# The first latent product issued before the change of blocks, in a decoder step on one core

## The reference

```python
def sq_relu_mlp(x, w_up, w_down):
    h = jax.nn.relu(x @ w_up)
    return (h * h) @ w_down

def shared_kv(h, pos, norm_kv, w_dkv, kv_norm, w_kr):
    hn = rmsnorm(h, norm_kv)
    ckv = rmsnorm(hn @ w_dkv, kv_norm)
    krope = rope(hn @ w_kr, pos)
    return ckv, krope
...
        h = h + sq_relu_mlp(rmsnorm(h, p["norm_mlp"][layer]), p["w_up"][layer], p["w_down"][layer])
        if layer == N_A_LAYERS - 1:
            ckv, krope = shared_kv(h, pos, p["norm_kv"], p["w_dkv"], p["kv_norm"], p["w_kr"])
```

## Time and profile before

| | us |
|---|---|
| median of 3 runs | 2909.66 |
| lowest and highest | 2902.77 and 2913.35 |
| the profiled execution | 2903.06 |
| its span in the trace | 2901.3 |
| TensorE busy in the span | 2766.8 (95%) |
| VectorE, ScalarE, GpSimd busy | 1455.0, 800.2, 736.6 |
| mean granted TensorE clock | 0.984 of full |

### The profile page before, as it was taken

The page is one execution under the profiler, slowest core; times in us unless marked ns, Lnnn a source line. Parts: engine busy times, 40 slices in busy tenths (PEclk is TensorE's granted clock), DMA queues, the critical chain, the costliest instruction groups (busy, mean ns, idle before and its releaser), DMA issues. The chain is left out here.

```text
span 2901.3 us, 54265 instructions
## 1 busy us (share of the span) xinstructions
PE 2766.8 (95%) x22530; PEld 2622.4 (90%) x22530; DVE 1455.0 (50%) x2072; ACT 800.2 (28%) x1349; POOL 736.6 (25%) x533
## 2 busy tenths in 40 slices
PE   6999999989899999999998999899999999999998
PEld 5988889978899999999997889767798999999997
DVE  6566666556743433334546666355466444424243
ACT  3122222223434430101213444333234333210101
POOL 2100000013434433333331110012134443333231
PEclk8999999999999999999999999999999999999998
DMA  4111111122233352322111001376222333532221
GB/s 113 46 58 57 54 54 54 45 84 83 84 108 103 106 205 74 103 93 90 38 39 45 31 27 35 127 266 272 67 96 93 111 97 114 185 105 79 103 73 73
DMA packets 244473, 267.48 MB, mean 92 GB/s; under 512 B 26320, under 2 KB 204288, under 8 KB 242208
## 3 DMA queue, kind: packets, MB, share of 16 engines
q1 hardware_dynamic: 208896, 207.34, 21.9%
q0 software_dynamic: 4608, 41.95, 3.7%
q10 hardware_dynamic: 30752, 14.99, 2.0%
HBM read 204.66 MB, written 59.57 MB: 91 GB/s over the span
## 5 line engine op out<-in xcount | busy, mean ns | idle before, releaser
L2083 DVE TENSOR_TENSOR h<-h,G 128x1050 f32<-128x1050 f32 x120 | 149.7, 1248 | 440.8 <-PE G L232 440.8
L232 PE MATMUL G<-a_hi,w_hi 128*128 128x350 f32 x1536 | 331.0, 323 | 0.0
L232 PE MATMUL G<-a_lo,w_hi 128*128 128x350 f32 x1536 | 330.9, 323 | 0.0
L232 PE MATMUL G<-a_hi,w_lo 128*128 128x350 f32 x1536 | 330.4, 323 | 0.0
L171 POOL CAST w_hi<-w_raw 128x1024 fp32r<-128x1024 f32 (+2 forms) x84 | 77.5, 922 | 731.9 <-PEq L1234 477.8
L232 PEld LDWEIGHTS G<-a_hi,w_hi 128*128 128x128 f32 x1536 | 262.8, 189 | 0.0
L232 PEld LDWEIGHTS G<-a_hi,w_lo 128*128 128x128 f32 x1536 | 262.0, 189 | 0.0
L232 PEld LDWEIGHTS G<-a_lo,w_hi 128*128 128x128 f32 x1536 | 261.3, 189 | 0.0
L1784 PE MATMUL G<-T_lo,wS_hi 128*128 128x262 f32 x768 | 219.9, 286 | 10.1 <-DVE T_lo L1940 10.1
L1784 PE MATMUL G<-T_hi,wS_hi 128*128 128x262 f32 x768 | 218.9, 285 | 0.0
L1784 PE MATMUL G<-T_hi,wS_lo 128*128 128x262 f32 x768 | 218.6, 285 | 0.0
(11 more groups left out here) (444 smaller groups left out, 6291.3 us busy)
## 6 DMA issues: line engine op xcount, KB each, us to landing
kept_a<-ring SPq DMA_DIRECT2D x128, 262.0 KB, 2.5
a_raw<-kept_a SPq DMA_DIRECT2D x64, 524.0 KB, 5.5
w_raw<-in_w_down SPq DMA_DIRECT2D x64, 512.0 KB, 3.5
wA_raw<-in_w_up SPq DMA_DIRECT2D x96, 256.0 KB, 3.3
wS_raw<-in_w_up SPq DMA_DIRECT2D x32, 256.0 KB, 3.8
kept_h<-h SPq DMA_DIRECT2D x14, 525.0 KB, 6.3
h<-kept_h SPq DMA_DIRECT2D x14, 525.0 KB, 6.8
w_raw<-in_hg_wq SPq DMA_DIRECT2D x8, 512.0 KB, 4.1
```

The costliest lines, as they stand in the source:

```text
L232: last = nc.tensor.matmul(out, w(a, t), x(b, t, c), start=(t == 0 and (a, b) == ORDER[0]), stop=(t == nk - 1 and (a, b) == ORDER[-1]))
L2083: nc.vector.tensor_tensor(h, h, tile(k, (g0 + t) % 2), ALU.add).then_inc(k.g_free, 1)
```

## The change

The first latent product and its norm product are issued at the end of the feed-forward block, right behind the feed-forward stage's last product, and no longer as the first thing of the `latents` block. GpSimd scales and splits the second latent weight block in the feed-forward block too. The loads of both blocks stood there already. Nothing is added or taken away.

```diff
         split_blocks(k, pool, W_GROUP * GROUPS, n0=self.w0)
         if self.latent_next:
-            split_scaled(k, pool, self.w_next, P, k.g_kv[:, :], k.n_scaled + 1)
+            for j in range(2):
+                split_scaled(k, pool, self.w_next + j, P, k.g_kv[:, :], k.n_scaled + 1 + j)
...
         if self.latent_next:
             pe.wait_ge(k.g_done, self.g_last + KD)
             pe.sem_inc(k.w_used, 1)
+            g = self.g_last + KD
+            first_product(k, pe, self.w_next, g + 1, 0, (g + 1) % 2, act_parts(self.x_hi, self.x_lo), self.x_next,
+                          KD, P, lambda: norm_pe(k, pe, KD, k.rstd, g, self.sq_next))
...
-    assert w0 % 2 == 0 and not k.w_held
+    assert w0 % 2 == 0 and k.w_held
...
-                for j in range(1, 6):
+                for j in range(2, 6):
                     width, gain = ROPE if j == 2 else P, k.g_kv[:, :] if j <= 2 else k.g_mix[:, 1, :]
                     split_scaled(k, pool, w0 + j, width, gain, k.n_scaled + 1 + j)
...
-                first_product(k, pe, w0, g0 + G_C, 0, (g0 + G_C) % 2, x, x0, KD, P,
-                              lambda: norm_pe(k, pe, KD, k.rstd, g0 + G_NORM, sq0))
                 product(1, G_C + 1)
```

## The result

The median is 2916.25 us over 12 runs (2908.55 to 2917.31), before 2909.2 us in the 12 runs of that series; the ratio is 1.0024, 95% interval 1.0014 to 1.0034. So the changed kernel is a little slower and inside the 0.5% that I took for no difference. Two later series of the same two kernels gave 1.0003 (0.9987 to 1.0018) and 1.0007 (0.9996 to 1.0018); both intervals exclude the 1.0024 of the first. Over all 32 runs of the changed kernel the mean is 2913.0 us, over the 76 runs of the kernel before in the same three series 2909.3: **+3.7 us**, with a standard error of 0.8. I had forecast +3.85 and 2913. That the mean comes so close is partly luck: by themselves the three series gave +6.9, +2.1 and +2.3 us.

A forecast was written before the change was run, and what follows sets the result against it. TensorE was busy for 95% of the span, so only its idle time and low clock could change. A later second product, +2.07, and its cold restart, +1.78, made +3.85 us on the median 2909.66: 2913 us, range 2903 to 2919.

The forecast's parts named there:

- The exchange comes later, and ScalarE is ready for the root 7.48 us behind it: Feed-forward block's end: exchange tied to TensorE's end, 1454.06 instead of 1445.08; clears and loads hold the root until 1461.54.
- The first product runs at the full clock after 1.37 us: Feed-forward block's end: TensorE's gap shrinks from 6.41 to 1.37 us; product and norm product take 13.56 us at full clock.
- The second product starts 2.07 us later: Latents block: the second product waits for the root and starts at 1462.87 instead of 1460.80, +2.07 us.
- Cold restart, +1.78: Second latent product: TensorE's 8.8 us idle before it drops the clock, so it starts slowly, +1.78 us.
- The second block's split costs nothing under its cover: Feed-forward block: GpSimd's split delays VectorE by 2.2 us, still ahead of TensorE's need; cost nothing, cover about 3 us.
- Rival 1: Exchange at the feed-forward block's end: TensorE's part doesn't wait for the array, root ready 3.1 us earlier; +0.8 us, chance 0.07.
- Rival 2: Latents block's head: clears and loads don't hold the root; second product follows a 1.6 us gap without clock loss; -5.1 us, chance 0.06.
- So the shift stays: From the second product on: TensorE has no slack to absorb the delay, so the whole +3.85 us remains.

The follow-up runs named there:

- the run that kept the clock up: The changed kernel with 14 useless matmuls on TensorE ahead of the second latent product: 2913.36 us, ratio 1.0013.
- two variants: The changed kernel with the second block's split back in the latents block (2915.29 us, 1.002), and with GpSimd's clears behind its write of rot (2912.95 us, 1.0011).
- The experiment without the cover: The kernel before with only the second latent block's scaling and split moved ahead of the exchange, the product left: 2913.8 us, ratio 1.0019.
- The kernel with the gap of 0.48 us: The changed kernel with the root in the feed-forward block and VectorE's release and reciprocal ahead of its memsets: 2903.72 us, ratio 0.9981.
- its control: The kernel before with the root of the norm ahead of the seven constant loads: 2909.13 us, ratio 0.9999.

## Why the prediction was right, point by point

- *The exchange comes later, and ScalarE is ready for the root 7.48 us behind it.* Right: the loads' last issue ended 1462.21 - 1454.71 = 7.50 us behind the product. Moving the clears made the gap 2.5 us shorter, moving the root in front of the loads made it 7.1 us shorter, and the same edit in the kernel before gave nothing. This step is shown.
- *The first product runs at the full clock after 1.37 us.* Right, 1.39, and in all nine profiles in which the product is moved.
- *The second product starts 2.07 us later.* From the end of the feed-forward stage it was 1460.80 - 1439.13 = 21.67, now 1463.58 - 1439.71 = 23.87: 2.20 later.
- *Cold restart, +1.78.* Right in kind, a little high: 1.58, 1.68 and 1.59 us in the three profiles of the changed kernel, and 1.6 by the run that kept the clock up. The 2.20 of the step above and 1.58 are 3.78, the forecast sum 3.85: the two misses cancel nearly. In two variants, profiled once each, it was 2.43 and 2.84, so the term is not a constant.
- *The second block's split costs nothing under its cover.* Right for the gap, which was 8.87 us with the split in either place. The experiment without the cover gave its price there: the 2.2 us of the gap, some 4.6 in the mean, of which the profile accounts for 4.0.
- *Rival 1, an exchange that doesn't wait for the array.* TensorE's drain of 3.88 us says no once more.
- *Rival 2, the way to a faster kernel.* The mechanism was right and its clock term wrong: with a gap of 1.78 us the cold start stayed. I had priced it at -5.1; the kernel with the root ahead came to 7.0 below the changed kernel, that is -3.3 by the profile. The kernel with the gap of 0.48 us had no cold start.
- *"So the shift stays."* At the place and through the prompt's attention it did. But I had not foreseen that a later block has its own luck with the clock, larger than my sum (1013.3 to 1024.3 us over all profiles). The first series' 1.0024 against the 1.0013 that I had is of that size. That the forecast met the mean of three series is thus partly luck, while the 3.7 us at the place are in all three profiles of the changed kernel. Whether the change itself makes the longer stretches likelier is open. Three profiles of the changed kernel were all at the long end (1023.3, 1023.4, 1024.3), three of the kernel before or its control at 1013.3, 1017.7 and 1021.1. But those three executions are of the changed kernel's upper group, to which only half of its runs belong. The counts lean the same way (6 of 20 and 10 of 12 runs, against 9 of 76) and differ too much between series to show it.

## What to carry to other kernels

Work moved ahead of a point where all engines meet shortens one engine's wait there and uncovers whatever the others have at the head of the next block. Before moving it, list for each engine what it does first behind that point, and for the result that the moved work hands over, how soon its consumer can run: here one square root behind seven load issues decided the sign, and an early root turned +3.7 us into -4.3 and -5.0 (ahead of the loads, two series) and -5.9 (in the feed-forward block), as means. A gap on TensorE costs its length and, in these profiles behind 1.78 us and behind 6.4 to 8.9 us, a slow restart too; the gaps of 0.48, 1.39 and 1.61 us cost their length alone.

A difference of 4 us in 2900 is also smaller than what one later block gave and took by itself. Here the stretch around the edit, read in several profiles, said more than the median of one series.

## What the runs showed of the hardware that I had not expected

- Short gaps at the two ends of block read here: 1.39 us left the granted clock at 1.00 in all nine profiles that have it, and 1.61 us ahead of the last block in all thirteen. 1.78 us, with one of 1.39 us 15 us earlier, dropped it both times, although it is only 0.17 us longer. Whether the length or what stood around the gap decided is not shown.
- The stretch at half clock after a restart was 3.5 to 6.2 us long with nearly the same work behind it (1.58 to 2.84 us lost).
- At the start of the sample attention the clock was 0.91, 0.81 or 0.70 over the same 40 us, although TensorE was busy for 36.7 to 36.9 of them in each case. By estimate, twice what is missing to 1.00 times 40, that is 7, 15 or 24 us at the half clock. The latter two have 8 and 17 us more than the first. Half of that, 4 and 8 us, is most of the 4.4 and 10.0 us by which the block was longer. What decides between the three is open.
- VectorE's low part of x took 3.4 to 3.5 us instead of 1.25 whenever GpSimd's subtraction ran beside it, in all kernels (48 times in the 13 profiles between 1405 and 1450 us).
